# Hyena filter spectra: one spectrum of forward and mirrored backward taps, with stacked low and high factors

## The chip, the cores and the metric

The kernel runs on one core of one Trainium2 chip. The metric is the device time of one launch in microseconds (us); lower is better. All data is float32, and every large product is made from three TensorE passes over parts with short mantissas (high times high, high times low, low times high).

## The reference

One encoder layer is applied to two sequences that are laid behind each other, 2048 rows (sample) and 256 rows (prompt), 1024 wide. What matters here is the long convolution of the Hyena mixer, 512 channels:

```python
h_f, h_b = implicit_filter(L, ...)       # (L, 512) each: sin MLP, 64 hidden, times a decay
k = concatenate([h_f, zeros((1, C)), h_b[:0:-1]])
U = rfft(u, n=2 * L);  K = rfft(k)
y = irfft(U * K, n=2 * L)[:L] + u * d_skip
```

The forward taps `h_f` reach into the past, the backward taps `h_b` (without tap 0) into the future. The rest of the layer is RMSNorm, one input projection 1024 to 2304, a three tap convolution, windowed attention, the output projection and a SwiGLU of width 2816.

## The kernel before

The first 850 us are the function `front`. Two programs are woven on every engine by `woven`: after each piece of the **main course** (the input projection: 54 units of 128 columns, two chunks of 384 rows each, called events 0 to 107) comes one piece of the **side program** (`side`), the filters and the Fourier work. One such pair is called a slot here; a slot of the main course has 12 TensorE passes of 386 columns, and there are 222 slots. Every engine runs its own instructions in this fixed order, so an engine that waits in one piece holds back everything behind it, the other program's too. DMAs are issued by SyncE (queue SP) and by GpSimd (queue POOL), in their own place in the same order. Transposes for `u_rows` wait for GpSimd's product L855, whose input VectorE makes (L1637).

The transform of length 4096 is split into 16 residues n2 of 128 rows each and a 16 point step between them. The side program has these stages:

- **Waves** (`wave`, `wave_mid`, `wave_end`): the two sine layers of the filter MLP, on 64 partitions. GpSimd first builds `w3`, the sum and the difference of the forward and backward output weights (L862 to L865), and ScalarE and VectorE split it.
- **Filter** (`made_step(t)` and `weigh_step(t)`, one slot each, t = 0 to 18, about 85 to 260 us). TensorE makes the taps of tile t out of the features (two products of three passes, `L85` to `L87` with `fi_fhi`, `fi_flo`), VectorE multiplies them by the decay (L1711, L1716), ScalarE and VectorE split them into `hhi` (L1456) and `hlo` (L1705). The sum and the difference filter are then transformed apart: `transform(w)` makes w = 0 to 31, two for each residue, real and imaginary part each. Of part w even ScalarE copies the real and VectorE the imaginary half out of PSUM into `out` (L1446, L1694); of part w odd ScalarE copies both (L1446, L1449). `out` has two slots, so part w waits until part w-2 is stored. GpSimd stores each into `f_dram` (L886) and brings the table of the next residue (L872). Two tiles of the prompt follow (`prompt(k)`), with tables of their own (L877).
- **Eighths** (`eighth(t, c)`, t = 0 to 15, three slots each, about 270 to 440 us): the 16 point step. SyncE loads 1 MB per t from `f_dram` (`bring_a`, L717, tile `fs_a`, two t ahead), ScalarE and VectorE split it (L1474, L1726), TensorE makes for both c two products of three passes with the factors `g16`, the results go to `k_dram` (L908).
- After event 51 the **u steps** (forward transform of u, 16 residues), then the **product steps** (`product_step(j)`, j = 0 to 17, two slots each with `return_step`, about 550 to 728 us): SyncE loads the spectrum of step j in a real and an imaginary part of 256 KB, each as four DMAs (`bring_k`, L751, tile `sp_k`), and the spectrum of u as four (`bring_octet`, L761, tile `sp_a`). VectorE multiplies: L1783 with what TensorE has just made in `gen`, L1786 (`sp_pb`) with its crossed copy, which ScalarE makes (L1528, L1529). TensorE's product of step j+1 overwrites `gen` and waits for `sp_pb` of step j. The **z steps** (inverse transform) follow.

From 850 us on come attention, output projection and the SwiGLU, which the change doesn't touch.

```python
        for t in range(NOCT):          # in side
            eighth(t, 0)
            yield
            eighth(t, 1)
            yield
            yield
        while now[0] < 2 * NU + 3:     # main course not yet at event 51
            yield
        first_u()
```

## Time and profile before

| | us |
|---|---|
| three timed runs: median (lowest, highest) | 2766.39 (2761.66, 2766.82) |
| profiled execution: span, first to last instruction | 2763.3 |
| TensorE busy in it | 2650.5 |
| span up to the end of the z steps | about 850 |

The profile gives the profiled execution's span; its own launch time isn't listed beside it, so the runs' median, 3.1 us above the span, stands for what lies around. Busy time of TensorE counts a pass of 512 columns as 0.39 us though the next begins 0.23 us after it; start to start is what a pass costs. Idle time of an engine is named by what ended it.

### The profile page before, as it was taken

The page shows a single profiled execution, that of the slowest core. Times are in us where ns is not written, and L with a number is a line of the kernel's source. Part 1 is how long each engine was busy: PE and PEld are TensorE (multiplying, and loading weights), DVE is VectorE, ACT ScalarE, POOL GpSimd, SP SyncE. Part 2 cuts the span into 40 slices and gives each one's busy share as a digit, 9 for nine tenths or more (in the row PEclk, how much of TensorE's full clock was granted, in tenths as well). Part 3 has the DMA queues.
Part 4 walks back from the last instruction along what each step waited for, and adds up shares of the span by engine and source line. Part 5 has one row for each costly group of instructions (what it writes and reads, how often), then busy time and mean ns, then how long its engine had stood idle before and what let it go on. Part 6 is the DMA issues. An engine that isn't in the chain of part 4 may idle for free.

```text
span 2763.3 us, 39808 instructions
## 1 busy us (share of the span) xinstructions
PE 2650.5 (96%) x14013; PEld 2413.5 (87%) x14013; DVE 2130.9 (77%) x2536; ACT 1395.3 (50%) x2397; POOL 1231.9 (45%) x1194
## 2 busy tenths in 40 slices
PE   8999899988898999999999999899999989999998
PEld 6888898878797888887999999899999989999997
DVE  6765575577747777877888888888888898888887
ACT  5564554467646777774434344444334453434342
POOL 3545112122212444456677764455655444443443
PEclk9999999999998999999999999999999999999999
DMA  7698988788998445444544443553443355333332
GB/s 232 212 306 266 300 256 250 261 259 270 262 261 208 119 126 146 125 128 142 178 140 140 134 126 96 183 158 115 117 116 106 88 180 163 88 88 92 92 88 88
DMA packets 476541, 463.24 MB, mean 168 GB/s; under 512 B 55214, under 2 KB 377390, under 8 KB 476055
## 3 DMA queue, kind: packets, MB, share of 16 engines
q1 hardware_dynamic: 445848, 379.94, 47.1%
q0 software_dynamic: 30496, 80.76, 9.3%
q8 instruction: 113, 1.85, 0.3%
q14 instruction: 84, 0.69, 0.1%
HBM read 338.41 MB, written 122.18 MB: 167 GB/s over the span
## 4 chain that ended last, share of the span: by engine, by line
PE 80%; DVE 7%; DMA 5%; SPq 3%; issue 2%; ACT 1%; POOL 1%; ACTq 0%; POOLq 0%; DVEq 0%
PE ff_banks L85 17%; PE ff_banks L86 17%; PE ff_banks L87 17%; PE pr_acc L85 3%; PE pr_acc L86 3%; PE pr_acc L87 3%; PE am_mix L85 2%; PE am_mix L86 2%; PE am_mix L87 2%; PE pr_gen L85 2%; PE am_turn L2273 2%; PE pr_gen L87 1%; PE pr_gen L86 1%; SPq L751 1%; DMA xkeep_dram<-pr_xs 1%
## 5 line engine op out<-in xcount | busy, mean ns | idle before, releaser
L3408 DVE TENSOR_TENSOR ff_h<-ff_h,ff_banks 128x1536 f32<-128x1536 f32 x231 | 402.8, 1744 | 5.9 <-PE ff_banks L87 5.5
L3244 ACT COPY ff_r<-ff_banks 128x384 f32<-128x384 f32 x198 | 95.0, 480 | 593.8 <-PE ff_banks L87 593.7
L3391 DVE TENSOR_TENSOR ff_dlo<-ff_dlo_raw,ff_dhi 128x512 fp32r<-128x512 f32 x231 | 213.6, 925 | 173.1 <-ACT ff_dhi L3274 173.0
L85 PE MATMUL ff_banks<-ff_xhi,ff_ghi 128*128 128x384 f32 x924 | 314.2, 340 | 13.9 <-DVE ff_silu L3368 8.1
L85 PE MATMUL pr_acc<-pr_xhi,pr_whi 128*128 128x386 f32 (+1 forms) x864 | 302.3, 350 | 13.1 <-DVE pr_xlo L1605 13.1
L87 PE MATMUL ff_banks<-ff_xhi,ff_glo 128*128 128x384 f32 x924 | 312.1, 338 | 0.0
L86 PE MATMUL ff_banks<-ff_xlo,ff_ghi 128*128 128x384 f32 x924 | 311.7, 337 | 0.0
L85 PE MATMUL ff_banks<-ff_xhi,ff_uhi 128*128 128x384 f32 x924 | 310.9, 336 | 0.9 <-ACT ff_r L3244 0.6
L86 PE MATMUL ff_banks<-ff_xlo,ff_uhi 128*128 128x384 f32 x924 | 310.6, 336 | 0.0
L87 PE MATMUL ff_banks<-ff_xhi,ff_ulo 128*128 128x384 f32 x924 | 310.0, 335 | 0.0
L3092 POOL TENSOR_TENSOR ff_act<-ff_act,ff_silu 128x384 f32<-128x384 f32 x99 | 117.0, 1182 | 419.3 <-issue 236.5
L86 PE MATMUL pr_acc<-pr_xlo,pr_whi 128*128 128x386 f32 (+1 forms) x864 | 295.4, 342 | 0.0
L87 PE MATMUL pr_acc<-pr_xhi,pr_wlo 128*128 128x386 f32 (+1 forms) x864 | 294.7, 341 | 0.0
L85 PE MATMUL ff_banks<-ff_dhi,ff_ahi 128*128 128x512 f32 x693 | 273.2, 394 | 9.7 <-issue 5.8
L86 PE MATMUL ff_banks<-ff_dlo,ff_ahi 128*128 128x512 f32 x693 | 273.3, 394 | 0.0
L87 PE MATMUL ff_banks<-ff_dhi,ff_alo 128*128 128x512 f32 x693 | 273.2, 394 | 0.0
L3395 DVE TENSOR_TENSOR ff_alo<-ff_act,ff_ahi 128x384 fp32r<-128x384 f32 x225 | 250.6, 1114 | 0.0
L85 PEld LDWEIGHTS ff_banks<-ff_xhi,ff_ghi 128*128 128x128 f32 x924 | 174.1, 188 | 22.1 <-DVE ff_silu L3368 9.1
L85 PEld LDWEIGHTS pr_acc<-pr_xhi,pr_whi 128*128 128x128 f32 x864 | 165.4, 191 | 23.5 <-DVE pr_xlo L1605 15.1
L86 PEld LDWEIGHTS ff_banks<-ff_xlo,ff_ghi 128*128 128x128 f32 x924 | 174.3, 189 | 5.9
L85 PEld LDWEIGHTS ff_banks<-ff_xhi,ff_uhi 128*128 128x128 f32 x924 | 173.3, 188 | 5.8 <-ACT ff_r L3244 0.9
L86 PEld LDWEIGHTS ff_banks<-ff_xlo,ff_uhi 128*128 128x128 f32 x924 | 173.5, 188 | 4.3
(330 smaller groups left out, 6820.2 us busy)
## 6 DMA issues: line engine op xcount, KB each, us to landing
ff_glo_raw<-w_gate_up SPq DMA_DIRECT2D x132, 256.0 KB, 3.0
ff_ulo_raw<-w_gate_up SPq DMA_DIRECT2D x132, 256.0 KB, 3.0
ff_dlo_raw<-dsum_dram SPq DMA_DIRECT2D x132, 256.0 KB, 2.7
pr_raw<-w_in SPq DMA_DIRECT2D x108, 256.0 KB, 6.0
ff_dlo_raw<-w_down SPq DMA_DIRECT2D x99, 256.0 KB, 2.6
f_dram<-fi_out POOLq DMA_DIRECT2D x32, 512.0 KB, 5.5
fs_a<-f_dram SPq DMA_DIRECT2D x32, 512.0 KB, 8.1
sp_k<-k_dram SPq DMA_DIRECT2D x128, 128.0 KB, 3.4
```

The source lines that it names most:

```text
L85: pe.matmul(out, still[0], moving[0], start=start, stop=False, skip_group_check=goes_on)
L86: pe.matmul(out, still[0], moving[1], start=False, stop=False, skip_group_check=goes_on)
L87: return pe.matmul(out, still[1], moving[0], start=False, stop=stop, skip_group_check=goes_on)
L751: sp.dma_start(hk[64 * d:64 * d + 64, u % 3, c], quads(k_dram[t], c)[:, :, o:o + HY]).then_inc(hk_in[u % 3], 16)
L2273: last = pe.transpose(turn[:, b, j * P:(j + 1) * P], prob[:, half_index(n, 4 * half) % 3, j, kb * P:(kb + 1) * P], ident[:])
L3092: pool.tensor_tensor(block, block, silu[c][:], ALU.mult).then_inc(tempered, 1)
L3244: act.copy(kept[n][:], bank(X)).then_inc(copied, 1)
L3391: dve.tensor_tensor(dlo[d_slot(n)][:], din[d_slot(n)][:], dhi[d_slot(n)][:].bitcast(F32), ALU.subtract).then_inc(d_low, 1)
L3395: dve.tensor_tensor(alo[n % AR][:], acts[:, STILL[k]], ahi[n % AR][:].bitcast(F32), ALU.subtract).then_inc(a_low, 1)
L3408: dve.tensor_tensor(to, to, lowered_all(k), ALU.add).then_inc(added, 1)
```

## The change

- The MLP's second layer is made twice, on partitions 0 to 63 and 64 to 127 (weights `w2` side by side). ScalarE rounds all 128 rows of a feature tile into `parts2`, VectorE replaces the lower 64 by the rest: high and low part of the features are stacked on the partitions, under output weights `w3` that stand twice. Two passes for a product in place of three (L1213, L1214 of the new file). The sums and differences of GpSimd and the clearing of `feat` go.
- Residues come in pairs n and 16-n (`ORDER`). `transform(n, c)` adds the forward taps of n and the mirrored backward taps of its partner into one spectrum: for c = 0 with the partner's cosines, for c = 1 with its negated sines (`minus`, which GpSimd makes from the table, L901). So there is one complex part per residue, not two. Six passes for each c; in all 192 as before. `hhi`, `hlo` and the table have four slots.
- `f_dram` is half as large: 16 stores of 512 KB in place of 32. ScalarE copies only the real half (16 copies and the prompt's 2, in place of 48 and 2), VectorE the imaginary half, one step later (`made_step(t)` copies that of residue t-4, `transform` of residue n runs at t = n+3).
- For the tiles 0, 16 and 17 VectorE gets extra steps (backward tap 0 cleared; for the prompt's the sum and difference that GpSimd's weights gave).
- The 16 point step gets its factors stacked (two 64 row blocks, `g4` to `g16`; that was done before the product steps): one product of three passes for each c, in place of two. An `eighth` takes two slots in place of three; SyncE brings t+4, as four DMAs of 128 KB.
- `k_dram` so comes out in an order that `bring_k` reads with two DMAs of 256 KB in place of four of 128 KB.

```diff
+    ORDER = [0, 8] + [n for k in range(1, 8) for n in (k, N2 - k)] + [N2, N2 + 1]
+    FIRST_OUT = 3
...
             eighth(t, 0)
             yield
             eighth(t, 1)
-            yield
             yield
         while now[0] < 2 * NU + 3:
...
+        def bring_a(t):
+            if t == 0:
...
+            if t >= 4:
+                sp.wait_ge(a_low, t - 3)
+            for c in range(2):
+                for d in range(2):
+                    sp.dma_start(sa[64 * d:64 * d + 64, t % 4, c], f_dram[:, 8 * t + 4 * c:8 * t + 4 * c + 4, HY * d:HY * d + HY]).then_inc(a_in[t % 4], 16)
...
-            for n in range(4):
-                bring_a(n)
+                sp.wait_ge(stored[s], 16 * (N2 // 2))
+            for t in range(4):
+                bring_a(t)
 
         def eighth(t, c):
-            if 2 * t + c + 4 < 2 * NOCT:
-                bring_a(2 * t + c + 4)
+            if c == 0 and t + 4 < NOCT:
+                bring_a(t + 4)
...
-            t, o = (u - 2) // 2, HY * (u % 2)
-            for c in range(2):
-                for d in range(2):
-                    sp.dma_start(hk[64 * d:64 * d + 64, u % 3, c], quads(k_dram[t], c)[:, :, o:o + HY]).then_inc(hk_in[u % 3], 16)
+            t, o = (u - 2) // 2, 64 * (u % 2)
+            for d in range(2):
+                sp.dma_start(hk[64 * d:64 * d + 64, u % 3].rearrange("p c x -> p (c x)"), k_dram[t, o:o + 64, :]).then_inc(hk_in[u % 3], 16)
...
+        def negate(n):
+            pool.wait_ge(table_in[n % 2], 16 * (n // 2) + 16)
+            pool.tensor_scalar(minus[:, n % 4], slot(table, n)[:, :, P:2 * P].bitcast(F32), -1.0, None, ALU.mult).then_inc(negated, 1)
...
         def made_step(t):
-            if 3 <= t:
-                store_part(2 * (t - 3) + 1)
-                pool.wait_ge(spectral, 4 * (t - 3) + 4)
-                bring_table(t - 1)
+            if t == 1:
+                pool.wait_ge(w3_low, 1)
+                for n in range(2):
+                    negate(n)
+            if t > FIRST_OUT:
+                store_part(t - FIRST_OUT - 1)
+            if t == 3:
+                pool.wait_ge(waved, 4)
+                for n in range(2, 4):
+                    bring_table(n)
+            if t >= 5 and t % 2:
+                pool.wait_ge(spectral, pair_done(t - 5))
+                for n in (t - 1, t):
+                    bring_table(n)
 
         def weigh_step(t):
-            if 2 <= t < N2 + 2:
-                store_part(2 * (t - 2))
+            if 4 <= t <= N2 and t % 2 == 0:
+                for n in (t - 2, t - 1):
+                    negate(n)
+            if t == 6:
+                stack()
 
...
+        def transform(n, c):
+
+            m = partner(n)
+            if c == 0:
+                for i in {n, m}:
+                    pe.wait_ge(table_in[i % 2], 16 * (i // 2) + 16)
+                pe.wait_ge(h_low, max(n, m) + 1)
+            else:
+                pe.wait_ge(negated, m + 1)
+            if n:
+                pe.wait_ge((copied_a, copied_v)[c], n)
+            own, other = slot(table, n), slot(table, m)
+            ahead = (own[:, 0, c * P:(c + 1) * P], own[:, 1, c * P:(c + 1) * P])
+            back = (minus[:, m % 4, 0], minus[:, m % 4, 1]) if c else (other[:, 0, 0:P], other[:, 1, 0:P])
+            triple(pe, gen[:, 2 + c, :], ahead, (slot(hhi, n)[:, 0], slot(hlo, n)[:, 0]), True, False)
+            triple(pe, gen[:, 2 + c, :], back, (slot(hhi, m)[:, 1], slot(hlo, m)[:, 1]), False, True).then_inc(spectral, 1)
...
                 for d in range(2):
-                    last = triple(pe, gen[:, d, :], (fhi[:, t % 2], flo[:, t % 2]), (w3hi[:, d], w3lo[:, d]), True, True)
+                    pe.matmul(gen[:, d, :], parts2[:, t % 2], w3hi[:, d], start=True, stop=False)
+                    last = pe.matmul(gen[:, d, :], parts2[:, t % 2], w3lo[:, d], start=False, stop=True)
                 last.then_inc(made, 1)
...
-            pe.wait_ge(a_low, 2 * t + c + 1)
-            for n, (m, q) in enumerate((((0, 0), (2, 1)), ((1, 2), (0, 3)))[c]):
-                last = triple(pe, gen[:, 2 * (t % 2) + c, :], (g16[:, m, 0], g16[:, m, 1]), (sahi[:, t % 2, q], salo[:, t % 2, q]), n == 0, n == 1)
-            last.then_inc(eighths, 1)
+            pe.wait_ge(a_low, t + 1)
+            triple(pe, gen[:, 2 * (t % 2) + c, :], (g16[:, 0, 0], g16[:, 0, 1]), (sahi[:, t % 2, c], salo[:, t % 2, c]), True, True).then_inc(eighths, 1)
...
-            if 2 <= t < N2 + 2:
-                part_out(2 * (t - 2))
-
-        def weigh_step(t):
-            if 2 <= t < N2 + 2:
-                part_out(2 * (t - 2) + 1)
+            if FIRST_OUT <= t < N2 + FIRST_OUT:
+                part_out(t - FIRST_OUT, 0)
...
         def made_step(t):
             if t + 1 < NTT:
                 feature_low(t + 1)
-            if 2 <= t < N2 + 2:
-                part_out(2 * (t - 2))
+            if FIRST_OUT < t:
+                part_out(t - FIRST_OUT - 1)
...
+                dve.wait_ge(weighed, t + 1)
+                dve.wait_ge(summed_up, at)
+                dve.tensor_tensor(h[:, 1, :], h[:, 0, :], h[:, 1, :], ALU.subtract).then_inc(summed_up, 1)
+                dve.wait_ge(summed_up, at + 1)
+                dve.scalar_tensor_tensor(h[:, 0, :], h[:, 0, :], 2.0, h[:, 1, :], ALU.mult, ALU.subtract).then_inc(weighted, 1)

In all TensorE's list of instructions has 12774 rows in place of 12905. Three places show how instructions move. First ScalarE in one filter step, from one split of the taps (`fi_hhi`) to the next:

```order
L1456 CAST fi_hhi<-fi_h 128x1024
L1440 CAST fi_fhi<-fi_feat 128x128
L1446 COPY fi_out<-pr_gen 128x512
L1308 CAST pr_whi<-pr_raw 128x1024
L1446 COPY fi_out<-pr_gen 128x512
L1449 COPY fi_out<-pr_gen 128x512
L1377 ACTIVATE pr_cx<-pr_acc,pr_cw 128x384
```

and the change:

```order
L1488 CAST fi_hhi_a<-fi_h 128x1024
L1474 CAST fi_parts<-fi_feat 128x128
L1480 COPY fi_out<-pr_gen 128x512
L1388 COPY pr_ust<-pr_turned 128x384
L1415 ACTIVATE pr_cx<-pr_acc,pr_cw 128x384
```

Two of three copies out of `gen` have gone, and with them two of the three places at which ScalarE can wait for a store.

Second SyncE's queue in the product steps, two steps (`sp_k` is the filter's spectrum, `sp_a` that of u, `x_dram` a store of the main course):

```order
L653 DMA x_dram<-pr_cx 128x384
L751 DMA sp_k<-k_dram 64x1x512 x4
L761 DMA sp_a<-a_dram 64x1x512 x4
L751 DMA sp_k<-k_dram 64x1x512 x4
L653 DMA x_dram<-pr_cx 128x384
L751 DMA sp_k<-k_dram 64x1x512 x4
L761 DMA sp_a<-a_dram 64x1x512 x4
L751 DMA sp_k<-k_dram 64x1x512 x4
```

and the change:

```order
L784 DMA sp_k<-k_dram 64x1024 x2
L794 DMA sp_a<-a_dram 64x1x512 x4
L784 DMA sp_k<-k_dram 64x1024 x2
L670 DMA x_dram<-pr_cx 128x384
L784 DMA sp_k<-k_dram 64x1024 x2
L794 DMA sp_a<-a_dram 64x1x512 x4
L784 DMA sp_k<-k_dram 64x1024 x2
L670 DMA x_dram<-pr_cx 128x384
```

Two product steps and their two stores had 26 DMAs in this queue, and now have 18.

Third TensorE in a product step, around the three products of 2 columns that sum the squares of the attention heads (L1090, and L1120 in the new file); `sp_ahi` is the product step's operand, `sp_yhi` that of the return step:

```order
L86 MATMUL pr_acc<-pr_xlo,pr_whi 128x386
L87 MATMUL pr_acc<-pr_xhi,pr_wlo 128x386
L1097 MATMUL pr_turned<-pr_ident,pr_rt 128x128 x3
L1090 MATMUL pr_turned<-pr_ones,pr_sq 128x2 x3
L85 MATMUL pr_gen<-sp_ahi,pr_g_65 128x512
L86 MATMUL pr_gen<-sp_alo,pr_g_65 128x512
```

and the change:

```order
L86 MATMUL pr_acc<-pr_xlo,pr_whi 128x386
L87 MATMUL pr_acc<-pr_xhi,pr_wlo 128x386
L1127 MATMUL pr_turned<-pr_ident,pr_rt 128x128 x3
L1120 MATMUL pr_turned<-pr_ones,pr_sq 128x2 x3
L85 MATMUL pr_gen<-sp_yhi,pr_g_65 128x512
L86 MATMUL pr_gen<-sp_ylo,pr_g_65 128x512
```

The u, product and z steps all begin one slot earlier in the main course (slot 105 for `first_u` in place of 106), so the sums of the heads now stand ahead of the return step and no more ahead of the product step.

## Rows read from the trace of the kernel before

**Rows 1.** The page: span, and busy time of each engine

```profile
span 2763.3 us, 39808 instructions
...
PE 2650.5 (96%) x14013; PEld 2413.5 (87%) x14013; DVE 2130.9 (77%) x2536; ACT 1395.3 (50%) x2397; POOL 1231.9 (45%) x1194
```

**Rows 2.** Windows by stage; the header line names the columns

```profile
core 0: us, PE busy (x) PEld busy (x) DVE busy (x) ACT busy (x) POOL busy (x), PEclk, DMA share, GB/s
80.00:270.00 190.00, 177.33 (x906) 156.19 (x906) 125.81 (x179) 106.22 (x185) 96.86 (x148) 0.99 0.83 265
270.00:440.00 170.00, 157.61 (x849) 146.38 (x848) 110.92 (x141) 91.20 (x138) 33.67 (x40) 0.99 0.96 278
...
560.00:740.00 180.00, 154.61 (x794) 141.69 (x792) 139.88 (x180) 122.42 (x202) 39.38 (x70) 0.95 0.89 265
...
850.00:2763.00 1913.00, 1868.23 (x9890) 1708.86 (x9888) 1584.67 (x1788) 932.13 (x1616) 990.85 (x824) 0.99 0.43 127
```

**Rows 3.** Tile gen under TensorE: count, then duration ns min/median/max, first and last start

```profile
L85 PE MATMUL pr_gen<-fs_ahi,pr_g x64: 387/392/477, 279.5 to 437.7; 128*128 128x512 f32 x64
...
L85 PE MATMUL pr_gen<-fi_w3hi,fi_fhi x36: 387/396/472, 86.4 to 243.9; 128*128 128x512 f32 x36
```

**Rows 4.** Timeline of TensorE at 200 us: start us, duration us

```profile
200.01 0.39 PE L86 MATMUL pr_gen<-fi_w3lo,fi_fhi 128*128 128x512 f32 x1
200.24 0.39 PE L87 MATMUL pr_gen<-fi_w3hi,fi_flo 128*128 128x512 f32 x1
200.47 0.34 PE L85 MATMUL pr_acc<-pr_xhi,pr_whi 128*128 128x386 f32 x1
200.65 0.34 PE L86 MATMUL pr_acc<-pr_xlo,pr_whi 128*128 128x386 f32 x1
```

**Rows 5.** Waits, 560 to 740 us: total us, times, longest us

```profile
DVE sp_pb L1786 <- DMA sp_k<-k_dram: 26.1, 12, 4.0
...
PE pr_gen L85 <- DVE sp_pb L1786: 18.2, 12, 4.9
```

**Rows 6.** Tile sp_k, then DMA issues of 570 to 720 us

```profile
L751 SPq DMA_DIRECT2D sp_k<-k_dram x128: 514/594/1964, 533.7 to 711.3; - x128
...
sp_k<-k_dram SPq DMA_DIRECT2D x116, 128.0 KB, 3.3
...
sp_a<-a_dram SPq DMA_DIRECT2D x52, 128.0 KB, 3.0
```

**Rows 7.** Waits, 80 to 270 us

```profile
ACT fi_out L1446 <- DMA f_dram<-fi_out: 27.3, 12, 4.6
...
PE pr_turned L1047 <- ACT pr_ust L1350: 4.5, 1, 4.5
...
PE pr_gen L85 <- DMA fi_table<-t_p_fwd: 2.3, 2, 1.9
...
PE pr_gen L85 <- ACT fi_out L1446: 1.1, 3, 0.5
```

**Rows 8.** Waits, 270 to 440 us, and one window inside that stage

```profile
ACT fs_ahi L1474 <- DMA fs_a<-f_dram: 25.1, 10, 7.4
...
PE pr_gen L85 <- DVE fs_alo L1726: 3.1, 1, 3.1
...
320.00:335.00 15.00, 15.00 (x81) 14.23 (x80) 5.50 (x8) 4.17 (x7) 0.54 (x1) 1.00 0.99 330
```

**Rows 9.** Single lines: GpSimd L841 and L855, VectorE L1678 and L1716

```profile
L841 POOL TENSOR_TENSOR tw_blocks<-tw_blocks x28: 453/490/1577, 42.9 to 287.2; 128x128 f32<-128x128 f32 x28
...
L855 POOL TENSOR_TENSOR pr_cx<-pr_cx x24: 1009/1910/2051, 52.4 to 416.0; 128x384 f32<-128x384 f32 x20, 128x386 f32<-128x386 f32 x4
...
  DVE pr_cx L1637: 117.2, 23
...
L1678 DVE SCALAR_TENSOR_TENSOR fi_arg<-fi_turns,fi_arg x4: 1351/1772/2049, 53.6 to 83.7; 64x1152 f32<-64x1152 f32 x4
...
L1716 DVE TENSOR_TENSOR fi_h<-pr_gen,fi_dec x18: 672/681/683, 92.4 to 251.1; 128x512 f32<-128x512 f32 x18
```

317 lines of the change are left out of this document (158 added, 159 removed).

## Prediction

> **What bounds the kernel now.** I began with the busy times: TensorE is busy in 2650.5 of 2763.3 us, the next engine in 2130.9 [rows 1]. TensorE's passes overlap, so busy time hides small gaps, and the stages have to be read apart [rows 2]. From 850 us on TensorE has 1868 of 1913 us, and the change doesn't reach there. In the filter stage (80 to 270 us) it idles 12.7 us, in the eighths (270 to 440) 12.4 us, in the product steps (560 to 740) 25.4 us. So a pass that is taken away shortens the span by nearly its own cost, and the idle times say where more is to be had. What a pass costs is read from the timeline: one of 512 columns begins 0.23 us after the one before, one of 386 columns 0.18 us, though each is drawn 0.39 and 0.34 us long [rows 4].
>
> Next come the waits of the product steps. TensorE waited 18.2 us for VectorE's `sp_pb`, in 12 pieces, and `sp_pb` itself 26.1 us, also in 12, for the load of the spectrum [rows 5]. That load isn't short of bandwidth but of SyncE: each of its DMAs holds the queue for 0.594 us, and from 570 to 720 us 116 of them and 52 of the sister load `sp_a` were issued [rows 6], 168 x 0.594 = 100 of 150 us, before weights and stores of the main course.
>
> Last the waits of the two stages that the change rewrites: in the filter stage ScalarE waited 27.3 us for a store to leave `out`, and TensorE 4.5 us for a late ScalarE, 2.3 us for the prompt's table and 1.1 us for ScalarE's copies [rows 7]. In the eighths ScalarE waited 25.1 us for the load, TensorE 3.1 us at the start [rows 8]. The DMA share is 0.96 in this stage [rows 2]: it is the one stage in which transfers are near the bound.
>
> **The change part by part.** All terms are against the span of 2763.3 us.
>
> *Passes.* The features lose one pass of three in 36 products, the eighths half of 64 products of three passes [rows 3]: 36 + 96 = 132 passes. The transforms keep their count. At 0.229 us: **-30.2 us**. All of them stand in stages where TensorE is at work for over nine tenths, so I take the whole.
>
> *Product steps.* The four DMAs of each spectrum part become two of double size. Of 116 issues 58 go: 34 us of queue time in 150. What is left, 110 x 0.594 = 65 us and the main course's, fits between the steps, and `sp_pb` no longer waits for the load. The order rows show the sums of the heads ahead of the return step now; ScalarE and VectorE work on them while TensorE returns, which can't hold back `sp_pb`. Late next is VectorE itself: 139.9 us of work in 180 [rows 2], 85% once the stage takes 165 us, strictly in order. Of 18.2 us I leave 4: **-14 us**, bounds 0 and -18.2 and, were the lower clock (0.95 in this stage, rows 2) to go with the waits, -25. The rule of the Trainium skill that speaks against this stands in "DMA: Bandwidth & Descriptors", "Anatomy of one DMA": about 50 ns of sequencer dispatch per DMA, told there of GpSimd's path. By it 64 DMAs less would be 3 us of queue and this term near 0. The row of 0.594 us decides against it.
>
> *Filter stage.* ScalarE makes 16 copies in place of 48, and `out` is written once a step in place of twice, so a store has a whole step, (243.9 - 86.4) / 17 = 9.3 us [rows 3], to leave where it had half. VectorE's copy one step later eats half of that for its own half only. The prompt's second table is asked for before the prompt's first product. Of 7.9 us of TensorE's waits [rows 7] I take **-6.5 us**; bounds 0 and -7.9.
>
> *Start of the eighths.* The loads wait for 16 stores, no more for the prompt's two: of 3.1 us [rows 8] **-2 us**; bounds 0 and -3.1.
>
> *Rate of the eighths.* A slot moved 0.5 MB of these spectra (1 MB in, 0.5 MB out in three slots), and still does (0.5 and 0.5 in two), but a slot shrinks by one pass, 0.23 of 158 / 48 = 3.3 us [rows 3]. The share of 0.96 would rise by 7%. One window stood at 0.99 with 330 GB/s and TensorE busy in all of it [rows 8], and loads are now asked for four t ahead, not two. I take **+2 us**; bounds 0 and 32 x 0.23 = 7.4. The 16 slots that the eighths no longer fill run with the main course alone. SyncE has 32 DMAs more here, 19 us of queue in about 100 us, beside work that left it idle.
>
> *GpSimd.* It gains 16 negations of 128 x 256 and 4 small copies (8 went). The nearest row is L841, 128 x 128 at 0.490 us [rows 9], so 0.98 us each, 16 us in a stage where it idles 93 of 190 us [rows 2]. Behind them stands its product L855, for which TensorE's transposes wait; before that product it idles 117.2 us in 23 times, 5.1 us each [rows 9], and that is the cover. What it may cost is VectorE: L1678 took 1.351 us at best and 2.049 us at worst [rows 9], 0.7 us more beside a busy GpSimd. **+1 us**; bounds 0 and 16 x 0.7 = 11. "SBUF — State Buffer" of the Trainium skill ("SBUF: two separate sides") makes it stricter: a VectorE instruction with two SBUF inputs and a GpSimd one that reads SBUF exclude each other for the whole instruction. By it each negation could hold VectorE for all its 0.98 us, 16 us in all, though TensorE would feel only part; the spread of L1678 agrees in kind.
>
> *Tiles 16 and 17.* VectorE has two more steps of 128 x 512 (0.681 us, rows 9) and a few of one row before TensorE may overwrite the taps: **+1.5 us**; bounds 0 and 4.
>
> *Start of the u steps.* They begin one slot earlier, in which the main course runs alone (12 x 0.178 = 2.1 us), but the u rows arrive no earlier: **+1.5 us**; bounds 0 and 2.1.
>
> *Costed at nothing:* the stacked second wave layer (same columns, more partitions), the removed sums and clearing on GpSimd before 35 us (nobody's wait there is TensorE's), the larger constants (one DMA more), the eight small factor loads (5 us of SyncE's queue in the filter stage, used five slots later).
>
> Sum: -30.2 - 14 - 6.5 - 2 + 2 + 1 + 1.5 + 1.5 = **-46.7 us**, a span of 2716.6 us. The median of the runs, 2766.4, is 3.1 us above the span; the same on top gives **2719.7 us**.
>
> **The rivals.**
>
> *A, the product steps keep their waits.* ScalarE (122 of 180 us) and VectorE (140) are loaded almost as TensorE is, and with SyncE gone one of them takes the bound, the more so as all their work now falls in another half of the event. For it: 85% load in strict order. Against it: of `sp_pb`'s waits nearly all are named as the load, and VectorE's arrival isn't early by accident but by 26 us. It takes the -14 away: 2733.7 us.
>
> *B, transfers bound the eighths.* The 32 slots keep their 3.3 us, and the loads in 128 KB pieces of 2 KB rows go no faster than the old of 4 KB: 7.4 in place of 2, and as much again as late weights: 2719.7 + 5.4 + 7.4, about 2732 us. For it the share of 0.96, against it the 330 GB/s.
>
> *C, waits go with their consequences.* The whole idle of the product steps beyond what its transitions need (25.4 in place of 14) and the rest of the filter's waits: 2719.7 - 11.4 - 1.4, about 2707 us.
>
> *D, slower: GpSimd is late for TensorE.* The second product of each of the 16 residues waits for `negated`. GpSimd comes to it in order, behind block sums, a store that waits for VectorE's later copy, and a table's landing. If TensorE waits there as it did at worst for `sp_pb`, 4.9 us [rows 5], that is 16 x 4.9 = 78 us: 2798 us. It decides from 46.7 / 16 = 2.9 us per residue. Against it: each negation stands two slots, half of 9.3 us, or more ahead of its use, and GpSimd idles half the stage.
>
> *E, the change doesn't do what it says*, no pass fewer: the order rows rule it out, since TensorE's list falls from 12905 to 12774 rows.
>
> **How the numbers follow.** Forecast 0.63, A 0.14, B 0.08, C 0.08, D 0.05, and 0.02 for an outcome within 0.2% (5.5 us, about what a measurement of this kernel can tell from no change) by several small mishaps. Faster by more than that: 0.63 + 0.14 + 0.08 + 0.08 = 0.93; same 0.02; slower 0.05. The range reaches down past C to the sum of the lower bounds (-30.2 - 25 - 7.9 - 3.1 = -66, taken four fifths of the way from the forecast: 2704) and up past A and B to 2738; D lies outside.
>
> **What would show it.** TensorE with 13,881 passes in place of 14,013. `sp_k` with 64 issues at about 0.6 us, the wait of `sp_pb` for the load under 5 us in all, TensorE's idle in the product steps near 10 us. ScalarE's wait for a store of `f_dram` under 8 us. In the eighths a slot near 3.1 us and TensorE waiting under 8 us for all loads and splits together. TensorE's wait for GpSimd's negations near zero: if it is over 10 us, D has begun. The forecast is wrong if the span of the stage from the first product step to the last doesn't shrink, or if the eighths' slots stay at 3.3 us.

## The result, and the profile after

| | before | after |
|---|---|---|
| runs, median (lowest, highest), us | 2766.06 (2761.66, 2766.82) | 2744.27 (2741.25, 2746.98) |
| span of the profiled execution, us | 2763.3 | 2745.2 |

The changed kernel takes 0.9924 of the time, 95% interval [0.991, 0.9938]: 21.8 us faster by the medians, 18.1 us by the two spans, where 46.7 us were forecast. 2744.3 us lies above the forecast's range (2704 to 2738). The page of the changed kernel opens with:

```profile
span 2745.2 us, 39433 instructions
...
PE 2624.6 (96%) x13881; PEld 2392.4 (87%) x13881; DVE 2117.1 (77%) x2526; ACT 1361.2 (50%) x2347; POOL 1229.5 (45%) x1182
```

The passes went as counted: 13,881 in place of 14,013 [rows 1]. Where the time went is read from the starts of TensorE's products on each tile, stage by stage (differences of these starts in the two profiled executions, us; "last" is the start of the last pass, and `sp_ahi` stands for a product step):

| stretch | before | after | change | forecast |
|---|---|---|---|---|
| filter: first feature product to first eighth | 193.1 | 189.9 | -3.2 | -14.2 |
| first eighth to first u step | 166.0 | 142.9 | -23.1 | -20 |
| first u step to first product step (`sp_ahi`) | 123.6 | 135.0 | +11.4 | +1.5 |
| first to last product step (`sp_ahi`) | 141.9 | 135.4 | -6.5 | -14 |
| last `sp_ahi` to last z step | 132.3 | 136.9 | +4.6 | 0 |
| start, and all after the z steps | | | -1.3 | 0 |

Three stretches missed: the filter stage, the way from the u steps into the product steps, and the product steps. The 23.1 us of the eighths look better than forecast, but this stretch also holds one slot of the main course less, at least 2.1 us that only moved behind it. Ten of the kernels below have as many slots there as before, and take 145.9 to 150.4 us: 15.6 to 20.1 us less.

The windows of the changed kernel, one for each stage (core 0: length, busy time of TensorE, of its weight loads, of VectorE, ScalarE and GpSimd with their instructions, granted clock, DMA share, GB/s):

```profile
85.80:275.70 189.90, 174.22 (x882) 156.05 (x882) 130.46 (x182) 85.06 (x147) 106.93 (x155) 0.96 0.79 238
276.00:376.00 100.00, 95.80 (x529) 89.79 (x527) 64.47 (x85) 56.46 (x89) 22.11 (x32) 0.98 0.86 288
553.00:690.00 137.00, 126.99 (x656) 114.03 (x655) 108.21 (x133) 96.90 (x158) 25.09 (x49) 0.97 0.98 266
```

The windows of [rows 2] don't begin and end with the stages, so here are the filter stage and the product steps of the kernel before once more, from their first product to their last:

```profile
86.40:279.50 193.10, 179.31 (x917) 158.12 (x918) 123.14 (x175) 103.39 (x180) 98.17 (x154) 0.99 0.85 269
569.00:711.00 142.00, 123.70 (x650) 112.74 (x649) 108.21 (x134) 99.50 (x162) 26.16 (x50) 0.98 0.87 264
```

In the filter stage TensorE idles 15.7 us where it was 13.8, with fewer passes to do, and the clock fell from 0.99 to 0.96. In the product steps it idles 10.0 us where it was 18.3, and the DMA share rose from 0.87 to 0.98. While the eighths run, the DMA share is 0.86 in place of 0.96, with 288 GB/s in place of 278 [rows 2]. From 850 us on all is as it was (TensorE 1851 of 1895 us). The waits of the filter stage, 80 to 276 us (engine, tile and line <- what ended the wait: us in total, times, longest):

```profile
POOL f_dram L907 <- DVE fi_out L1722: 48.9, 13, 10.1
...
ACT fi_out L1480 <- DMA f_dram<-fi_out: 4.7, 1, 4.7
PE pr_gen L85 <- DMA fi_table_b<-t_p_fwd: 4.7, 1, 4.7
...
PE pr_gen L1213 <- DVE fi_parts L1716: 3.5, 1, 3.5
...
PE pr_gen L1213 <- DVE fi_h L1769: 2.7, 1, 2.7
PE pr_gen L85 <- DVE fi_out L1722: 2.6, 2, 1.5
PE pr_gen L1213 <- DVE fi_h L1749: 2.6, 1, 2.6
...
PE pr_gen L85 <- DVE fs_alo L1773: 0.7, 1, 0.7
```

ScalarE's wait for a store fell from 27.3 us to 4.7 [rows 7], and the start of the eighths from 3.1 to 0.7 us [rows 8], as forecast. But GpSimd now waits 48.9 us for VectorE's later copy, and TensorE 4.7 us for the prompt's second table, 3.5 + 2.7 + 2.6 = 8.8 us for VectorE's work on features and taps, and 2.6 us for its copies. (The wait of 3.5 us ends with the first feature product, at 85.8 us; the other two stand at tile 17 and tile 1.) None of the negated tables is waited for.

The waits around the product steps, 550 to 710 us:

```profile
DVE sp_pb L1830 <- DMA sp_k<-k_dram: 12.7, 6, 3.0
...
PE pr_gen L85 <- DVE sp_pb L1830: 7.5, 5, 3.7
...
DVE sp_pa L1827 <- DMA sp_k<-k_dram: 4.7, 2, 3.0
```

The load is still waited for: `sp_pb` 12.7 us in place of 26.1 [rows 5], both products together 17.4 where they waited 29.5 before. TensorE waits 7.5 us for `sp_pb` in place of 18.2. The issues of the spectrum, and the transfers of 553 to 709 us with their time from issue to landing:

```profile
L784 SPq DMA_DIRECT2D sp_k<-k_dram x64: 445/596/5641, 505.7 to 686.4; - x64
```

```profile
sp_k<-k_dram SPq DMA_DIRECT2D x58, 256.0 KB, 6.0
...
sp_a<-a_dram SPq DMA_DIRECT2D x52, 128.0 KB, 5.2
```

An issue holds SyncE as long as before, 0.596 us, for twice the bytes. With half the issues SyncE has room: in the product steps it now waits 51.3 us for other engines, where it waited 11.9 us before. But a DMA of the spectrum lands after 6.0 us in place of 3.3, and the untouched `sp_a` after 5.2 in place of 3.0 [rows 6]. Last, the waits of 500 to 560 us, where 11.4 us were lost:

```profile
PE pr_acc L85 <- DVE pr_xlo L1633: 11.6, 2, 6.1
```

Here the main course waits for its own splits `pr_xlo`; before the change it did so once, for 2.8 us, in the same part of the course.

### The profile page after: what moved, and what is told of

Read it like the earlier page. It is cut to its first block, busy times and chain, and to the rows that moved or that the text cites. A ratio compares the mean times of both kernels' runs of the same rounds, so it can differ in the third digit from the quotient of the medians.

```text
span 2745.2 us, 39433 instructions
## 1 busy us (share of the span) xinstructions
PE 2624.6 (96%) x13881; PEld 2392.4 (87%) x13881; DVE 2117.1 (77%) x2526; ACT 1361.2 (50%) x2347; POOL 1229.5 (45%) x1182
## 4 chain that ended last, share of the span: by engine, by line
PE 81%; DVE 8%; DMA 3%; issue 2%; SPq 2%; ACT 1%; POOL 1%; ACTq 0%; DVEq 0%; POOLq 0%
PE ff_banks L85 17%; PE ff_banks L86 17%; PE ff_banks L87 17%; PE pr_acc L85 4%; PE pr_acc L86 4%; PE pr_acc L87 4%; PE am_mix L85 2%; PE am_mix L87 2%; PE am_mix L86 2%; PE am_turn L2317 2%; PE pr_gen L85 1%; PE pr_gen L86 1%; PE pr_gen L87 1%; DMA sp_k<-k_dram 1%; PE am_acc L2331 1%
## 5 line engine op out<-in xcount | busy, mean ns | idle before, releaser
L85 PE MATMUL pr_acc<-pr_xhi,pr_whi 128*128 128x386 f32 (+1 forms) x864 | 304.4, 352 | 24.0 <-DVE pr_xlo L1633 23.6
L85 PE MATMUL ff_banks<-ff_xhi,ff_ghi 128*128 128x384 f32 x924 | 313.5, 339 | 12.2 <-DVE ff_silu L3412 6.5
L87 PE MATMUL ff_banks<-ff_xhi,ff_glo 128*128 128x384 f32 x924 | 311.6, 337 | 0.0
L85 PE MATMUL ff_banks<-ff_xhi,ff_uhi 128*128 128x384 f32 x924 | 310.8, 336 | 0.6 <-ACT ff_r L3288 0.6
L86 PE MATMUL ff_banks<-ff_xlo,ff_ghi 128*128 128x384 f32 x924 | 311.1, 337 | 0.0
L86 PE MATMUL ff_banks<-ff_xlo,ff_uhi 128*128 128x384 f32 x924 | 310.6, 336 | 0.0
L87 PE MATMUL ff_banks<-ff_xhi,ff_ulo 128*128 128x384 f32 x924 | 310.0, 335 | 0.0
L86 PE MATMUL pr_acc<-pr_xlo,pr_whi 128*128 128x386 f32 (+1 forms) x864 | 297.5, 344 | 0.0
L87 PE MATMUL pr_acc<-pr_xhi,pr_wlo 128*128 128x386 f32 (+1 forms) x864 | 296.8, 344 | 0.0
L85 PE MATMUL ff_banks<-ff_dhi,ff_ahi 128*128 128x512 f32 x693 | 273.6, 395 | 9.7 <-issue 5.8
L86 PE MATMUL ff_banks<-ff_dlo,ff_ahi 128*128 128x512 f32 x693 | 273.6, 395 | 0.0
L87 PE MATMUL ff_banks<-ff_dhi,ff_alo 128*128 128x512 f32 x693 | 273.2, 394 | 0.0
L85 PEld LDWEIGHTS pr_acc<-pr_xhi,pr_whi 128*128 128x128 f32 x864 | 166.6, 193 | 34.9 <-DVE pr_xlo L1633 26.1
L85 PEld LDWEIGHTS ff_banks<-ff_xhi,ff_ghi 128*128 128x128 f32 x924 | 173.7, 188 | 20.5 <-DVE ff_silu L3412 7.4
L86 PEld LDWEIGHTS ff_banks<-ff_xlo,ff_ghi 128*128 128x128 f32 x924 | 173.8, 188 | 5.9
L85 PEld LDWEIGHTS ff_banks<-ff_xhi,ff_uhi 128*128 128x128 f32 x924 | 173.3, 188 | 5.2 <-ACT ff_r L3288 0.9
L86 PEld LDWEIGHTS ff_banks<-ff_xlo,ff_uhi 128*128 128x128 f32 x924 | 173.5, 188 | 4.3
## 6 DMA issues: line engine op xcount, KB each, us to landing
ff_glo_raw<-w_gate_up SPq DMA_DIRECT2D x132, 256.0 KB, 3.0
ff_ulo_raw<-w_gate_up SPq DMA_DIRECT2D x132, 256.0 KB, 2.9
ff_dlo_raw<-dsum_dram SPq DMA_DIRECT2D x132, 256.0 KB, 2.7
pr_raw<-w_in SPq DMA_DIRECT2D x108, 256.0 KB, 5.4
ff_dlo_raw<-w_down SPq DMA_DIRECT2D x99, 256.0 KB, 2.6
sp_k<-k_dram SPq DMA_DIRECT2D x64, 256.0 KB, 6.2
```

Source lines behind the costliest of these rows:

```text
L85: pe.matmul(out, still[0], moving[0], start=start, stop=False, skip_group_check=goes_on)
L86: pe.matmul(out, still[0], moving[1], start=False, stop=False, skip_group_check=goes_on)
L87: return pe.matmul(out, still[1], moving[0], start=False, stop=stop, skip_group_check=goes_on)
```

## The experiments

Stage lengths in this section are worked out as in the table above, from each run's own trace. The filter stage's code is the same in the changed kernel and six runs (parity, spread, k4, k_half, prod_place, two_slots): 187.5 to 190.1 us, mean 189.4. That is its scatter. Nearly all of it lies at the stage's start: from TensorE's first transform product to the first eighth the seven take 166.7 to 168.7 us, mean 167.1.

### The place of the later steps

The change also removed one of the three slots of each eighth. The side work waits for a fixed event of the main course before the u steps; with one slot less at the end of the eighths everything from there on had moved by one slot, which is half an event.

```
parity:                              before_early (the kernel before):
             yield                               eighth(t, 1)
+            yield                               yield
             first_u()                      +    if t:
                                            +        yield      (was: yield)
```

> The changed kernel with one empty slot more ahead of the first u step, so that the u, product and z steps stand at the same half of the main course's event as in the kernel before. Theory 'place': the 11 us that the changed kernel loses between the first u step (26.9 us early) and the first product step (15.5 us early) come from VectorE's main splits falling behind the octets' splits, because all steps moved by half an event. Then TensorE's stalls from 500 to 560 us fall from 16.2 to about 6.5 us, and the run takes 2733 to 2737 us, 8 to 11 under the changed kernel's 2744. Rival 'transfers': the first octets' loads are late because all transfers were brought forward by 25 us onto the weights; then the place does nothing, 2743 to 2747 us, and the stalls stay at 14 us or more.

> The kernel before with one empty slot less in the eighths, so that its u, product and z steps stand half an event earlier, as in the changed kernel; nothing else is altered. Theory 'place': slower than before by 8 to 11 us, 2774 to 2777 us, with stalls from 520 to 580 us of some 16 us in place of 6.5. Rival 'transfers': 2764 to 2768 us, as before.

Measured: parity 2732.23 us (2728.59 to 2736.53), 12 us faster than the changed kernel; before_early 2782.36 (2778.47 to 2783.44) against 2765.57 for before, ratio 1.0059 [1.0046, 1.0072], 16.8 us slower by nothing but one empty slot less. (Its slot is left out behind the first eighth, so the other eighths moved too.) The place costs, in either kernel, and more than I had put down. From the first u step to the first product step: 124.3 us in parity, 132.9 in before_early, where 123.6 (before) and 135.0 (after) had been; the products and the way to the last z step took 2.6 and 4.5 us less in parity than in the changed kernel, though kernels with the same code and place as parity scatter by more than that there (product steps 131.3 to 137.4 us). Parity loses 7.5 us of this by starting its u steps later. TensorE's waits for `pr_xlo` in this part of the course show the same: 11.6 us (changed) and 11.7 (before_early), twice about 6 us, against one wait of 4.0 us in parity.

What VectorE does there, in its timeline. The changed kernel (start us, length us, line, what; in brackets the idle time before):

```profile
528.84 1.22 DVE L1820 TENSOR_TENSOR sp_pb<-sp_k,pr_gen 128x1024 f32<-128x1024 f32 x1 [0.70 <-PE pr_gen L87]
531.31 1.26 DVE L1806 TENSOR_TENSOR sp_alo<-sp_a,sp_ahi 128x1024 fp32r<-128x1024 f32 x1 [1.26 <-ACT sp_ahi L1540]
532.50 2.36 DVE L1633 TENSOR_TENSOR pr_xlo<-pr_xs,pr_xhi 128x512 fp32r<-128x512 f32 x2
...
541.46 1.22 DVE L1820 TENSOR_TENSOR sp_pb<-sp_k,pr_gen 128x1024 f32<-128x1024 f32 x1
542.60 1.22 DVE L1806 TENSOR_TENSOR sp_alo<-sp_a,sp_ahi 128x1024 fp32r<-128x1024 f32 x1
543.73 2.28 DVE L1810 TENSOR_TENSOR sp_ylo<-sp_yf,sp_yhi 128x1024 fp32r<-128x1024 f32 x1
545.94 2.35 DVE L1633 TENSOR_TENSOR pr_xlo<-pr_xs,pr_xhi 128x512 fp32r<-128x512 f32 x2
```

And parity. Its lines are numbered one higher:

```profile
539.51 2.49 DVE L1634 TENSOR_TENSOR pr_xlo<-pr_xs,pr_xhi 128x512 fp32r<-128x512 f32 x4
...
543.24 1.21 DVE L1821 TENSOR_TENSOR sp_pa<-sp_k,pr_gen 128x1024 f32<-128x1024 f32 x1
544.37 1.21 DVE L1821 TENSOR_TENSOR sp_pb<-sp_k,pr_gen 128x1024 f32<-128x1024 f32 x1
545.50 1.22 DVE L1807 TENSOR_TENSOR sp_alo<-sp_a,sp_ahi 128x1024 fp32r<-128x1024 f32 x1
546.64 2.30 DVE L1811 TENSOR_TENSOR sp_ylo<-sp_yf,sp_yhi 128x1024 fp32r<-128x1024 f32 x1
```

At the change of round (the main course takes up its next group of row tiles) VectorE owes it a row of splits. In the changed kernel the second octet's whole load (`sp_pb`, `sp_alo`, `sp_ylo`) stands ahead of the last of them; in parity the splits come first. TensorE then stops twice, and its clock goes too. 530 to 554 us in the changed kernel, then in parity (columns as above):

```profile
530.00:536.00 6.00, 1.69 (x5) 1.69 (x6) 4.74 (x6) 5.76 (x8) 3.47 (x2) 0.66 0.78 236
536.00:542.00 6.00, 6.00 (x25) 5.48 (x25) 2.96 (x4) 1.25 (x3) 0.28 (x1) 0.78 1.14 279
542.00:548.00 6.00, 1.54 (x9) 1.22 (x7) 6.00 (x5) 0.85 (x3) 4.66 (x3) 0.79 1.06 349
548.00:554.00 6.00, 4.40 (x13) 4.36 (x14) 1.58 (x5) 0.00 (x0) 0.00 (x0) 0.50 0.08 18
```

```profile
530.00:536.00 6.00, 6.00 (x29) 5.48 (x29) 3.57 (x5) 0.00 (x0) 2.26 (x2) 0.88 0.39 118
536.00:542.00 6.00, 3.30 (x16) 2.43 (x14) 4.77 (x7) 5.86 (x11) 0.86 (x2) 0.97 0.77 219
542.00:548.00 6.00, 4.70 (x15) 4.70 (x16) 5.96 (x8) 0.88 (x1) 2.33 (x2) 0.50 1.06 367
548.00:554.00 6.00, 6.00 (x32) 5.66 (x31) 3.37 (x5) 2.95 (x5) 2.09 (x1) 0.96 0.96 281
```

52 passes in 24 us against 92. A granted clock of 0.50 is the lower level, 1.2 GHz; each time TensorE had stood idle for several us just before (4.5 us of the 6 before 548 in the changed kernel; a wait of 4.0 us in parity).

Two more runs take the place apart:

```
prod_place:  + yield behind the 16 u steps, ahead of the product steps
two_slots:   + yield, yield ahead of first_u()
```

> The changed kernel with the extra empty slot behind the u steps, not ahead of them: u steps at the new place, product and z steps at the old one. Theory: it is VectorE's work for the first two octets (products, split, split of y) against the splits of the round change that costs, so the product steps' place decides and the whole 12 us of parity come back: 2731 to 2734 us. Rival: the u steps' own place costs (their last split waits behind the main course); then 2738 to 2744 us.

> The changed kernel with two empty slots ahead of the u steps: the same half of an event as in the changed kernel, one whole event later. Theory 'half of the event': what matters is in which half of each event VectorE meets the side work, so this is as slow as the changed kernel, 2742 to 2748 us. Rival 'distance to the round change': the side steps were too early against the change of round, and any later place is good: 2731 to 2736 us.

Measured: prod_place 2729.38 us (2727.95 to 2732.82), two_slots 2742.27 (2739.07 to 2745.58). So it isn't the u steps' place but that of the products and z steps, and it isn't the distance to the round change but the half of the event: one slot later helps, two slots later don't. In prod_place the main course waits once for its splits, 4.0 us, as in parity. In two_slots the wait of the main course for its splits is back:

```profile
PE pr_acc L85 <- DVE pr_xlo L1635: 11.9, 2, 7.0
```

### The product steps: issues or bytes

```
(both on top of parity, inside the loop over the two halves d of the partitions)
k4:     for c in range(2): sp.dma_start(hk[64d:64d+64, u % 3, c], k_dram[t, o:o+64, HY*c:HY*(c+1)])
k_half: for d in range(2 if u < 5 else 1): (as in the changed kernel)
```

> parity (the changed kernel with one more empty slot), but each part of a spectrum from u = 2 on is read by four DMAs of 128 KB in place of two of 256 KB; same bytes, 64 issues of SyncE more. Theory 'SyncE binds the product steps': sp_pb waits again for its load by some 25 us in all, the stretch from the first to the last sp_ahi product grows from 132.8 to 139 us or more, and the run by 6 to 10 us, to 2738 to 2742 us. Rival 'transfers bind': the issues were hidden, the stretch stays within 2 us and the run at 2732 us.

> parity, but from the sixth part of a spectrum on only the lower 64 partitions are loaded (one DMA of 256 KB, not two; the upper 64 keep an older part, so this leaves half of the loads out). Theory 'transfers bind what is left': the DMA share of the product steps falls from about 1.0 to 0.7, the waits of sp_pb and sp_pa for loads go, and the run gets 4 to 8 us faster, 2724 to 2728 us. Rival 'VectorE and ScalarE bind': the loads were only the last of several that arrive together; 0 to 2 us, 2730 to 2732 us.

| first to last product step | us | run, us |
|---|---|---|
| parity | 132.8 | 2732.23 |
| k4 | 140.6 | 2736.56 (2730.54 to 2741.17) |
| k_half | 120.9 | 2720.73 (2712.94 to 2723.99) |

The waits of 540 to 700 us, first in k4, then in k_half:

```profile
DVE sp_pb L1832 <- DMA sp_k<-k_dram: 23.8, 10, 3.6
PE pr_gen L85 <- DVE sp_pb L1832: 15.8, 11, 2.3
```

```profile
DVE sp_pb L1831 <- ACT sp_crossed L1558: 11.3, 16, 0.7
...
PE pr_gen L85 <- DVE sp_pb L1831: 1.6, 2, 1.0
```

(k_half leaves half of the loads out, so it doesn't compute the convolution.) *k4*: 64 issues cost 7.8 us of this stage against parity, 0.12 us each where the queue is held for 0.6. Seven other kernels with the product steps of parity, at its place (third, no_negate, nocomb, spread, best1, best3, prod_place), take 131.3 to 137.4 us, so k4's 140.6 is outside the scatter, but the size is known to a few us only, and the whole run lost 4.3, with ranges that overlap. SyncE's own waits agree that the issues bind there: over the product steps it waits 9.3 us for other engines in k4, 44.0 in parity.

*k_half*: the waits for the load vanish, and the stage takes 12 us less. A DMA of the spectrum lands after 4.7 us in place of 5.9. But this run halved the issues (29 of 58) together with the bytes, and a run with half the bytes and all the issues wasn't made. That the bytes are what counts is argued from SyncE's 44.0 us of room in parity, and the DMA share of parity (1.05 from 549 to 682 us, 281 GB/s) points the same way. The share alone doesn't decide: I expected it to fall to 0.7, and it is 0.97 in k_half, at 251 GB/s, with nobody waiting for the load. So behind the queue the stage had a second bound close by, by all signs the time that transfers take to land, and my -14 assumed one.

### The filter stage

The edits, the last three on top of parity. third adds the low part of the taps twice, no_negate leaves a sign out, and nocomb leaves out the extra steps of tiles 16 and 17, so none of the three computes the right filter:

```
copy_now:      VectorE's part_out(t - 3) at the end of weigh_step(t), not part_out(t - 4) in made_step(t)
tables_first:  GpSimd: bring_table(N2 + 2), (N2 + 3) ahead of store_part(N2 - 1)
third:         + pe.matmul(gen[:, d, :], parts2[:, t % 2], w3lo[:, d]) a second time
no_negate:     - the 16 pool.tensor_scalar(minus...), and the wait for them
nocomb:        if t: in place of  if t not in (0, N2, N2 + 1):
```

> The changed kernel with VectorE's copy of each imaginary half in the same step as its product (as ScalarE's copy of the real half), not a step later. Theory 'chain': in the filter stage the store, GpSimd behind it and the prompt's tables are late through the late copy (GpSimd waits 48.9 us for it in 13 stores, TensorE 4.8 us for the prompt's table). Then these go: GpSimd's wait for VectorE under 20 us, the prompt's wait near 0, and the filter stage 4 to 6 us shorter, 2738 to 2740 us. Rival 'VectorE in order': a copy placed earlier holds VectorE for TensorE's second product, and its splits of the taps and the main course come later: filter stage 0 to 5 us longer, 2744 to 2749 us.

> The changed kernel; GpSimd asks for the prompt's two tables before it stores the last residue, not behind that store, which waits for VectorE's late copy. Theory 'chain': TensorE's wait of 4.8 us for this table at 256 us shrinks to 1 us or less, and the run by 3 to 4 us, to 2740 us. Rival 'TensorE absorbs it': the wait returns as one for the splits of the last tiles, 2743 to 2745 us.

> parity, with the third pass of the feature products back (here a repeat of the pass with w3lo, so the taps' low part is counted twice): 36 passes more, all in the filter stage. My term: a pass is worth its 0.229 us, so the stage from the first feature product to the first eighth (189.7 us in parity) grows by 8.3 us and the run by as much, to 2740 us. Rival 'chain': the stage is set by waits along VectorE and ScalarE, and the passes fill idle time: 0 to 4 us, 2732 to 2736 us.

> parity without GpSimd's negated tables: the second product of each residue takes the table as it is (the sign of one term is left out). My term for the negations was 1 us (bounds 0 and 11). Theory: GpSimd's 16 negations lengthen VectorE's splits beside them and bring the block sums late, so the stage falls by 2 to 5 us to 2727 to 2730 us. Rival: they cost nothing, 2731 to 2733 us.

> parity without VectorE's two combining steps at each of the last two feature tiles (the sum and difference of the heads, and the skip row of tile 16, are left out). TensorE's wait of 2.8 us at 233 us should go and that of 4.8 us for the prompt's table stay: 2 to 3 us faster, 2729 to 2730 us. Rival: the time returns as a longer wait for the table, 2732 us.

| | filter stage | from the first transform product on | run, us |
|---|---|---|---|
| the same code in seven kernels | 187.5 to 190.1 | 166.7 to 168.7 | |
| copy_now | 186.3 | 165.9 | 2741.46 (2739.41 to 2750.12) |
| tables_first | 186.6 | 166.2 | 2744.88 (2741.89 to 2745.89) |
| third | 196.9 | 174.0 | 2736.42 (2730.96 to 2737.47) |
| no_negate | 189.6 | 166.5 | 2730.15 (2726.61 to 2731.93) |
| nocomb | 183.6 | 161.7 | 2728.53 (2722.39 to 2735.12) |

*third* adds 36 passes and 7.5 us against the mean of 189.4, with 8.3 by the count and 0 to 4 by the rival. 30 of its passes stand behind the first transform product: 6.9 us by the count, 6.9 measured. So in this stage the passes taken away were worth their price; "the passes fill idle time" is refuted. The whole run lost 4.2 us, with ranges that overlap, and doesn't decide. *no_negate* finds nothing: the negations cost no time in this stage. *copy_now* and *tables_first* missed: from the first transform product on they gain about 1 us, and no time of the run that their scatter allows to claim. In copy_now GpSimd still waited 37.2 us for VectorE's copies, where I expected under 20, and TensorE 4.3 us for the table; in tables_first it was 3.7 us, since GpSimd may ask for the table only once the last residue's product is done. The late copy alone isn't what holds it.

*nocomb* found a large part of what was missing: 5.8 us under the mean, 5.4 from the first transform product on, where I had put 1.5 for these steps. The windows of 225 to 275 us in the changed kernel, and in nocomb:

```profile
225.00:275.00 50.00, 41.51 (x204) 36.95 (x203) 28.57 (x37) 15.46 (x24) 28.24 (x41) 0.93 0.78 220
```

```profile
225.00:275.00 50.00, 45.38 (x228) 40.54 (x228) 26.43 (x34) 16.63 (x26) 33.62 (x48) 0.97 0.87 248
```

TensorE's wait for `fi_h` at tile 17 (2.7 us) goes, the table's falls to 3.5, and the clock stays higher: 24 passes more in the same 50 us. The changed kernel shows how a wait and the clock belong together, first around the wait of 3.5 us for the first feature parts, then behind that of 4.7 us for the table:

```profile
78.00:82.00 4.00, 4.00 (x25) 3.94 (x23) 3.90 (x6) 3.88 (x6) 0.08 (x1) 1.00 0.72 204
82.00:86.00 4.00, 0.47 (x3) 0.25 (x2) 3.87 (x5) 2.47 (x5) 3.92 (x3) 0.84 0.00 0
86.00:90.00 4.00, 4.00 (x13) 3.51 (x14) 3.90 (x5) 0.48 (x1) 3.43 (x5) 0.50 0.24 69
90.00:94.00 4.00, 4.00 (x21) 4.00 (x19) 2.92 (x5) 0.00 (x0) 3.76 (x6) 0.81 0.22 62
...
260.00:266.00 6.00, 4.91 (x12) 3.91 (x13) 0.00 (x0) 0.59 (x1) 0.04 (x1) 0.53 0.87 279
```

TensorE is idle from 82 to 86 us, then makes 13 passes in 4 us at the lower level where it had made 25. Behind the wait of 2.7 us at tile 17 the clock stayed at 1.00. The start of the stage explains its scatter too: up to 110 us the clock is 0.80 to 0.82 in the five kernels that take 189.7 us or more, and 0.93 in the two that take 187.5 and 189.0.

### A version that beats both

best1 is parity with three edits, not tried one by one: VectorE's copy in the same step; the prompt's second table into the decay tile's memory, free by then; TensorE waits for VectorE's reads of PSUM at tiles 1 and 17, not for the combination in SBUF behind them.

```
+    ptab = Place(nc, "fi", dec_at).sb("ptab", [P, 2, 2, 2 * P], F32R)
+    if t in (1, N2 + 1): pe.wait_ge(weighed, t); pe.wait_ge(summed_up, 1 if t == 1 else 2)
     elif t: pe.wait_ge(weighted, t)
```

spread and best3 spread the eighths over three slots again, without and with these edits; best2 reads each part of a spectrum by one DMA whose source is read twice (`ap=[[0, 2], [2 * HY, 64], [1, 2 * HY]]`).

> parity, and three edits of the filter stage: VectorE copies the imaginary half in the same step; the prompt's second table goes to the decay tile's memory and is asked for before the prompt's first product; TensorE waits for VectorE's reads of PSUM, not for the combination behind them, at tiles 1 and 17. Theory 'chain': of the stalls of the filter stage (3.7, 2.8, 1.6, 2.8, 1.3, 4.8 us) the last goes and the second and fourth shrink by 1 to 2 us each, 8 us in all: 2724 us. Rival 'covered': TensorE meets the next late work (splits of the eighths' loads, main course) and half returns: 2728 to 2730 us.

> The changed kernel with an empty slot more in each of the 16 eighths (three slots an eighth, as before the change), which also puts the later steps back at their old half of the event. If the term for the eighths' rate was right (transfers cost up to 2 us in the dense form), this is 0 to 2 us faster than parity, 2730 to 2732 us. Rival: the idle slots at the end of the stage in parity serve to bring u rows and weights ahead; spread out they don't, and this is 1 to 4 us slower than parity, 2733 to 2736 us.

> The kernel of the run best1 with three slots an eighth in place of the one empty slot ahead of the u steps. By the runs spread and parity (2.4 us apart, within their scatter) it is 0 to 3 us faster than best1: 2721 to 2724 us. Rival: the same as best1 or up to 2 us slower, 2724 to 2726 us.

> The kernel of the run best1, and each part of a spectrum is read by one DMA of 512 KB whose source is read twice, in place of two of 256 KB. If SyncE's issues still cost something in the product steps, 29 fewer in 135 us give 1 to 4 us: 2720 to 2723 us. Rival 'transfers bind, in larger pieces': a part lands later as a whole (a DMA of 256 KB took 5.9 us, of 128 KB 3.6 us), and VectorE waits longer for it: 0 to 5 us slower, 2724 to 2729 us.

Measured: best1 2723.83 us (2721.12 to 2731.81), ratio to before 0.985 [0.9836, 0.9865]; best3 2722.13 (2720.72 to 2726.67), 0.9853 [0.9833, 0.9872]; spread 2729.84 (2724.28 to 2735.48). The filter stage of best1 takes 182.6 us, and the table's wait is down from 4.7 to 2.3 us; the wait for `fi_h` at tile 17 is gone:

```profile
PE pr_gen L1220 <- DVE fi_h L1757: 2.3, 1, 2.3
PE pr_gen L85 <- DMA fi_ptab<-t_p_fwd: 2.3, 1, 2.3
```

The same code in best3 and best2 takes 180.4 us. So the combination of tiles 16 and 17 can be kept without TensorE waiting for it at tile 17. Two or three slots an eighth makes no difference that these runs can tell. best1 and best3 take 42 and 41 us off the kernel before. best2 was a bad miss: 2975.47 us, 252 us slower than best1.

## Why the prediction was wrong

**Passes, -30.2 us: right for the features, about right for the eighths.** *third* priced the features' part at 7.5 us against 8.3. The eighths' 96 passes were to give 22.0 us, 20 with the term for the rate; with equal slots they gave 15.6 to 20.1. Where the rest went was not tried.

**Rate and start of the eighths, +2 and -2: right.** The start gave 2.4 us. A slot of the eighths took 3.4 us before (46 slots lie between the first and the last product, not the 48 that I divided by) and takes 3.2 now, one pass less. The DMA share fell from 0.96 to 0.86 in place of rising by 7%, at 288 GB/s, and spreading the slots again gained nothing that could be told. Why the same bytes a slot keep the DMA engines less busy was not tried. Rival B is out.

**Start of the u steps, +1.5 us: this is one of the two steps that failed most.** I priced one slot as time in which the main course runs alone, bounds 0 and 2.1 us, and left everything behind it at its old duration. The runs show 12 us (parity), all of it by the product and z steps falling into the other half of the event (prod_place, two_slots), where VectorE's octet work comes ahead of the main course's splits. My rival A names it in passing, "all their work now falls in another half of the event", and uses it only to take the gain of the product steps away, not to charge the main course.

**Product steps, -14 us: right mechanism, size too large.** They gave 6.5 us, and 9.1 in parity (4.5 to 10.6 with the scatter at the old place). SyncE's queue was the bound, and the row of 0.594 us was the right one to trust: k4 makes 64 issues worth 7.8 us of the stage. The Trainium skill ("DMA: Bandwidth & Descriptors", "Anatomy of one DMA") gives about 50 ns of sequencer dispatch, for GpSimd's path; by it the estimate was 3 us, and for SyncE the runs don't agree. But "that load isn't short of bandwidth" failed. The DMA share stood at 0.89 in this stage before [rows 2], which the prediction doesn't weigh; behind the queue the landing of a DMA went from 3.3 to 6.0 us, and 12 us more came only with half the bytes and half the issues. Rival A holds in part, and what takes over is, as far as k_half shows, the loads' landing: with it gone VectorE carries 109 of 121 us and holds TensorE 1.6 us.

**Filter stage, -6.5 us: this is the other step that failed most.** ScalarE's wait for stores went as forecast (27.3 to 4.7 us), and TensorE's wait for the late ScalarE fell from 4.5 to 1.1 us. But this term sums only old waits that go, and no new ones that come. TensorE's idle time in the stage rose from 13.8 to 15.7 us: it now waits for VectorE at tile 1 (2.6 us) and tile 17 (2.7), for VectorE's copies (2.6), and 4.7 us for the prompt's table in place of 1.9. It isn't that fewer passes leave less cover: in *third*, with the passes back, TensorE idles 14.8 us in the stage.

**Tiles 16 and 17, +1.5 us: mis-sized**, 5.4 to 5.8 us by nocomb. I added up two VectorE instructions, and left out that the prompt's table comes later behind them, and that TensorE comes back from that longer wait at a lower clock (0.53 from 260 to 266 us).

**The clock** was in no term of the filter stage, and belongs there: it fell from 0.99 to 0.96 in 190 us, which is up to 190 x 0.03 = 5.7 us of passes. How much of it is a loss beside the waits was not measured apart.

**Negations, +1 us: nothing.** By the rule of the Trainium skill on the shared port ("SBUF — State Buffer", "SBUF: two separate sides") my estimate let each hold VectorE for up to 0.98 us; no_negate shows the stage at 189.6 us against a mean of 189.4, so whatever VectorE lost wasn't on the path. Rival D is out: TensorE never waited for `negated`.

With the place restored the forecast's other terms give -46.7 - 1.5 = -48.2 us; parity gave 33.8. By parity's trace it fell short in the filter stage (11 us), the product steps (5) and the eighths (4), and got some 4 us back behind the z steps, where nothing was changed: that part scatters by 6 us between kernels. Rival C, with more gain than forecast, is out too, and so is E by the passes.

## What to carry to other kernels

Where two courses of work are woven slot by slot and one engine serves both in strict order, removing or adding a slot moves everything behind it: compare which of the two comes first on that engine at the busiest point, in the order of instructions, and price that rather than the slot. When a queue is the bound, look at what stands second: here the time that a load takes to land nearly doubled once the issues came faster. A list of waits that go is half a forecast; go through every instruction that the change adds or moves later, and ask who will wait for it. And price a wait of TensorE with the slower passes that may follow it: here 3.5 us of waiting cost another 12 passes.

## What the runs showed of the hardware that I had not expected

Doubling the size of the spectrum's DMAs left the issue at 0.6 us and the bytes the same, but moved the landing of the neighbours: `sp_a`, untouched, from 3.0 to 5.2 us (5.1 in parity), and back to 3.2 us in k4.

A DMA of 512 KB whose source is read twice by a zero stride was far slower than two of 256 KB that read the same bytes. The product steps took 359.6 us (133.5 in best1), the DMA share fell to 0.31, and VectorE's waits from 546 to 906 us were:

```profile
DVE sp_pb L1838 <- DMA sp_k<-k_dram: 164.7, 15, 12.2
...
DVE sp_pa L1835 <- DMA sp_k<-k_dram: 82.8, 14, 9.1
```

SyncE was held too, by the DMAs that come next in its queue, for up to 14 us, as in:

```profile
614.70 11.78 SPq L631 DMA_DIRECT2D pr_raw<-w_in  x1
```

For long parts of these holds little moves. Here is one such stretch, behind the issue of a spectrum load at 633.77 us, while SyncE was held from 634.33 to 641.49 us:

```profile
636.00:638.00 2.00, 2.00 (x12) 1.74 (x11) 0.00 (x0) 0.00 (x0) 0.00 (x0) 1.00 0.13 51
```

A share of 0.13 is that of 2 DMA engines of 16, and at 51 GB/s a load of 512 KB takes 10 us, about as long as SyncE is held. The single piece of 128 partitions isn't to blame: `pr_xs`, also 512 KB into 128 partitions by one DMA, landed after 6.5 us in best1. What is left is the source that is read twice, whose outermost dimension has just two entries; a load with the dimensions in another order was not tried.
